# A three-branch decoder step on one core: the norms' factors spread by rounded high and low parts in place of four-byte products

## Chip, cores and metric

The kernel runs on one core of a Trainium2 chip. The metric is the device time of one execution in microseconds, lower is better.

## The reference, cut to what matters

One layer on 1024 prompt tokens and 8 sample tokens (1032 columns here), width 1024, everything in float32: a SwiGLU feed-forward block, an RWKV-7 and an S5 branch that are merged by gates, a second SwiGLU block, and a last norm. In front of each block stands the same norm:

```
def rmsnorm(x, g):
    xf = x.astype(jnp.float32)
    y = xf * lax.rsqrt(jnp.mean(xf * xf, axis=-1, keepdims=True) + NORM_EPS)
    return (y * g.astype(jnp.float32)).astype(x.dtype)

x = x + 0.5 * swiglu(rmsnorm(x, g_ffn1), ffn1_gate, ffn1_up, ffn1_down)
h = rmsnorm(x, g_mix);  proj = h @ w_in
...
x = x + 0.5 * swiglu(rmsnorm(x, g_ffn2), ffn2_gate, ffn2_up, ffn2_down)
y = rmsnorm(x, g_final)
```

## The kernel before

Activations lie with the 1024 channels on the partitions (8 tiles of 128) and the 1032 tokens along the row. **Large products.** A weight tile and an activation are each split into a part rounded to the format fp32r and the rest, also rounded; a product is hi*hi + hi*lo + lo*hi, three TensorE matmuls of fp32r (`product`, L199, its matmul on L213; L3476 in the second feed-forward block, L3495 and L3541 in its second half). One matmul has 344 columns (a third of the tokens, BLK), or 258 at L3476. POOL splits the weights (L179, L182; L3159), SyncE loads them.

**The norms.** A norm's factor 1/rms belongs to a token, and so is one number per column, the same on all 128 partitions. It is not applied to the input of the products but to their outputs, by VectorE, from the tile `rstd` (128 x 1032). It is made in four steps:

- ScalarE squares, VectorE adds up the eight tiles of squares in `ssum` (`square_sum`, L265).
- `sums_pe` (L276, matmul on L282): 12 four-byte matmuls with 86 columns of `ssum` as the weights and a column of ones (`seg`, column 2) as the moving operand. They turn the sums so that 86 tokens lie on 86 partitions: `ps[0:86, 6, 0:12]`.
- `rstd_small_dve` (L300): VectorE copies these 86x12 numbers into `small` and takes the reciprocal root in twelve more small steps (L230 to L241, three Newton steps), each waiting for the one before it; the result is `small[:, 1]`. Then it raises `rstd_small`.
- `rstd_pe` (L287, matmul on L293): 12 four-byte matmuls, each with one column of `small` repeated 128 times as the weights (86 rows x 128 columns) and the 86x86 identity `ident` as the moving operand; the result is the factor of 86 tokens on all 128 partitions. VectorE copies them to `rstd` in three pieces (`rstd_dve`, L309, copy on L313).

This happens three times: in front of the first feed-forward block (norm 0; TensorE comes to `rstd_pe` ahead of its fourth unit of weights, L581), in the projections (norm 1; inside the second unit, ahead of its sixth tile, L349 to L352), and in the second feed-forward block (norm 2; the root is written out by hand between other VectorE work, L3248 to L3263, and TensorE comes to `rstd_pe` after the fourth product of the second pair, L3483). The last norm has a copy of the step of its own (`factors_pe`, L3698, matmul on L3701) that reads `small` and `ident` too.

**Order.** Each engine runs one written-out list of instructions in order. TensorE's list is `sums_pe`, more large products, `rstd_pe`, more large products; a product's operands are waited for by semaphores (`w_split` from POOL, `set_free` from the engine that empties a PSUM bank). `seg` and `ident` are loaded by SyncE once near the start (L3601, L3602), with the semaphore `c_in`, for which TensorE waits on L574. `small` is 128 x 6 x 16 numbers; its rows 0 to 2 are the root's x, y and t, row 5 is the constant zero, and rows 3 and 4 are free.

Of the kernel before, what the change touches and what calls it, by code (L numbers as in the profile page):

```python
# [4 lines left out]
F32 = mybir.dt.float32  # L5
F32R = mybir.dt.float32r
I32 = mybir.dt.int32
ALU = mybir.AluOpType
# [4 lines left out]
P = 128  # L13
# [18 lines left out]
J = 16  # L32
SS = 86
NSS = TOK // SS
L8 = 8
GATES = 16
NORM_EPS = 1e-6
# [14 lines left out]
T_SEG = 7  # L52
# [45 lines left out]
def plan(nc, g):  # L98

    base = (nc.sbuf_base + 31) // 32 * 32  # L100
    g.limit = nc.sbuf_usable_end - base

    def at(name, off, shape, dt=F32):
        t = nc.alloc_sbuf_tensor_at(name, shape, dt, offset=base + off)
        return t, off + (int(np.prod(shape[1:])) * 4 + 31) // 32 * 32

    g.at = at
    o = 0

    g.wraw, o = at("wraw", o, [P, WSLOTS, 1024])  # L110
    g.whi_off = o
    g.whi, o = at("whi", o, [P, WSLOTS, 1024], F32R)
    g.wlo_off = o
    g.wlo, o = at("wlo", o, [P, WSLOTS, 1024], F32R)
    g.vec_off = o
    g.vec, o = at("vec", o, [P, NVEC])
    g.ident, o = at("ident", o, [P, P])
    g.seg, o = at("seg", o, [P, P])
    g.small, o = at("small", o, [P, 6, 16])
    g.zero = g.small[:, 5, 0:1]  # L120
    g.rstd, o = at("rstd", o, [P, TOK])
    g.s5p, o = at("s5_persistent", o, [P, 4, J])

    g.hhi, o = at("hhi", o, [P, DT, TOK], F32R)
    g.hlo, o = at("hlo", o, [P, DT, TOK], F32R)
    g.h_end = o
    g.x, o = at("x", o, [P, DT, TOK])
    g.x_end = o
    ga = max(FFN_GROUPS)
    g.ahi, o = at("ahi", o, [P, ga, TOK], F32R)  # L130
    g.alo, o = at("alo", o, [P, ga, TOK], F32R)
    g.first_raw = at("first_raw", o - 2 * TOK * 4, [P, 2, TOK])[0]
    g.tmp_off = o
    g.tmp, o = at("tmp", o, [P, 2, TOK])
    g.ssum, o = at("ssum", o, [P, TOK])
    assert o <= g.limit, (o, g.limit)
    g.ffn_end = o
    g.ps = nc.alloc_psum_tensor("ps", [P, 8, 512], F32)

    S = nc.alloc_semaphore  # L140
    g.w_in = [S("weights_in0"), S("weights_in1")]
    g.w_hi = S("weights_hi")
    g.first_set = S("first_steps")
    g.w_split = S("weights_split")
    g.unit_done = S("unit_done")
    g.set_free = [S("set_free0"), S("set_free1")]
    g.dve_s, g.act_s, g.pool_s = S("dve_steps"), S("act_steps"), S("pool_steps")
    g.x_in, g.c_in, g.out_done = [S(f"x_in{k}") for k in range(DT)], S("consts_in"), S("out_done")
    g.sq_ready, g.ssum_step, g.norm_ss = S("squares_ready"), S("square_sums"), S("norm_sums")
    g.rstd_small, g.rstd_b, g.rstd_ready = S("rstd_small"), S("rstd_broadcast"), S("rstd_ready")  # L150
    g.hhi_ready, g.h_ready = S("h_hi"), S("h_ready")
    g.silu_done, g.a_full, g.a_hi, g.a_ready = S("silu_done"), S("a_full"), S("a_hi"), S("a_ready")
    g.dve_n = g.act_n = g.pool_n = 0
    g.units = 0
    g.uses = [0, 0]
    g.norms = 0
    g.a_tiles = 0
# [80 lines left out]
def rsqrt(v, st, y, x, t, scale, eps, floor=None):  # L238

    if floor is None:  # L240
        st.do(v.tensor_scalar(x, x, scale, eps, ALU.mult, ALU.add))  # L241
    else:
        st.do(v.tensor_scalar(x, x, scale, floor, ALU.mult, ALU.max))
    rsqrt_steps(v, st, y, x, t)
# [31 lines left out]
def sums_pe(pe, g, n, ssum=None):  # L276

    pe.wait_ge(g.ssum_step, DT * (n + 1))
    if n:
        pe.wait_ge(g.rstd_ready, 3 * n)  # L280
    for j in range(NSS):
        last = pe.matmul(g.ps[0:SS, 6, j:j + 1], (g.ssum if ssum is None else ssum)[:, j * SS:(j + 1) * SS], g.seg[:, 2:3],  # L282
# [4 lines left out]
def rstd_pe(pe, g, n):  # L287

    pe.wait_ge(g.rstd_small, n + 1)
    for j in range(NSS):  # L290
        if j == 10:
            pe.wait_ge(g.rstd_ready, 3 * n + 1)
        last = pe.matmul(g.ps[:, 6 + (j // 5) % 2, (j % 5) * SS:(j % 5 + 1) * SS],  # L293
                         g.small[0:SS, 1, j:j + 1].to_broadcast([SS, P]), g.ident[0:SS, 0:SS],
                         start=True, stop=True)
        if j in (4, 9, 11):
            last.then_inc(g.rstd_b, 1)


def rstd_small_dve(v, g, st, n):  # L300

    v.wait_ge(g.norm_ss, n + 1)
    x, y, t = (g.small[0:SS, a, 0:NSS] for a in range(3))
    st.do(v.tensor_copy(x, g.ps[0:SS, 6, 0:NSS]))
    rsqrt(v, st, y, x, t, 1.0 / D, NORM_EPS)
    v.sem_inc(g.rstd_small, 1)


def rstd_dve(v, g, n):  # L309
# [25 lines left out]
def h_dve(v, g, gcol, n):  # L335

    for k in range(DT):
        h_lo(v, g, gcol, n, k)
    for k in range(DT):
        square_sum(v, g, n, k)  # L340
# [22 lines left out]
def ffn_block(nc, g, w_up, w_down, gcol, before=None, after=None, setup=None, ahead=None, loaded=False, normed=False,  # L363
# [24 lines left out]
    if block:  # L388
# [37 lines left out]
        def _(v):  # L426
            st = Steps(v, g.dve_s, g.dve_n)
            if not normed:
                h_dve(v, g, gcol, n0)
            rstd_small_dve(v, g, st, n0)  # L430
            rstd_dve(v, g, n0)
            v.wait_ge(g.rstd_ready, 3 * n0 + 3)
# [2592 lines left out]
def strassen_ffn(nc, g, w_up, w_down, gcol, n0, a_dram, x_dram, final, update, updated, block):  # L3025
# [187 lines left out]
    def _(v):  # L3213
        st = Steps(v, g.dve_s, g.dve_n)
# [15 lines left out]
        def first_pairs():  # L3230
            G, U = ([[halves(t[:, j, x]) for x in xa] for j in range(2)] for t in (g.gate, g.upv))
            R = [halves(g.rstd[:, x]) for x in xa]
            x, y, t = (g.small[0:SS, a, 0:NSS] for a in range(3))

            def add(pair, k, copy, out, where):
                done(v, 0, pair, k)
                g.st_copy.wait(v, 0, pair, copy)
                return v.tensor_tensor(out, two(where, pair), out, ALU.add)

            def newton():  # L3240
                st.do(v.scalar_tensor_tensor(t, y, -0.5, y, ALU.mult, ALU.mult))
                st.do(v.tensor_tensor(t, t, x, ALU.mult))
                st.do(v.scalar_tensor_tensor(y, t, 1.5, y, ALU.add, ALU.mult))

            for q in range(4):
                late("b22", g.x[:, 2 * q + 1, xa[1]], q)
            v.wait_ge(g.norm_ss, n0 + 1)
            st.do(v.tensor_copy(x, g.ps[0:SS, 6, 0:NSS]))  # L3248
            st.do(v.tensor_scalar(x, x, 1.0 / D, NORM_EPS, ALU.mult, ALU.add))
            on(add(0, 3, "p1", G[0][0], "y"))  # L3250
            on(add(0, 4, "p5", U[0][1], "x"))
            st.do(v.tensor_scalar(t.bitcast(I32), x.bitcast(I32), 1, None, ALU.logical_shift_right))
            st.do(v.tensor_scalar(y.bitcast(I32), t.bitcast(I32), -1.0, RSQRT_MAGIC, ALU.mult, ALU.add))
            newton()
            on(add(0, 5, "u2", G[0][1], "z"))
            newton()
            done(v, 0, 0, 6)
            on(v.tensor_copy(U[0][0], two("x", 0)))
            newton()
            v.sem_inc(g.rstd_small, 1)  # L3260
            add(1, 3, "p1", G[1][0], "y").then_inc(g.b_mixed, 1)
            rstd_dve(v, g, n0)
            v.wait_ge(g.rstd_ready, 3 * n0 + 3)  # L3263
            g.st_up.wait(v, 0, 0, "u1")
            on(v.tensor_tensor(G[0][0], G[0][0], R[0], ALU.mult))
            on(v.tensor_tensor(G[0][1], G[0][1], R[1], ALU.mult))
            on(v.tensor_tensor(U[0][1], U[0][1], R[1], ALU.mult))
            add(1, 4, "p5", U[1][1], "x").then_inc(g.b_mixed, 1)
            v.tensor_tensor(U[0][0], U[0][0], R[0], ALU.mult).then_inc(g.b_mixed, 1)
            v.wait_ge(g.b_mixed, 19)  # L3270
            g.st_copy.wait(v, 0, 0, "silu1")
            on(v.tensor_tensor(G[0][0], G[0][0], U[0][0], ALU.mult))
            g.st_up.wait(v, 0, 0, "u2m")
            g.st_copy.wait(v, 0, 0, "silu2")
            on(v.tensor_tensor(G[0][1], G[0][1], U[0][1], ALU.mult))
# [48 lines left out]
        for u in range(LAST):  # L3324
# [8 lines left out]
            if k < 6:  # L3333
                t = 6 * b + k
                hi, low, full = g.slot[DOWN_BLOCKS[b + 1][2][k]]
# [229 lines left out]
def build(nc, a, o):  # L3565

    g = Ctx()
# [20 lines left out]
    def first_loads(sp):  # L3588
        def unit(n):
            sp.dma_start(g.wraw[:, n, :], a["ffn1_up"][n]).then_inc(g.w_in[n], 16)  # L3590

        def odd_x(ks):
            for k in ks:
                sp.dma_start(g.x[:, k, :], a["x"][:, k, :]).then_inc(g.x_in[k], 16)

        unit(0)
        odd_x((1, 3, 5))
        unit(1)
        odd_x((7,))
        sp.wait_ge(g.hhi_ready, 1)  # L3600
        sp.dma_start(g.ident[:, :], a["tabs"][:, T_ID, :]).then_inc(g.c_in, 16)  # L3601
        sp.dma_start(g.seg[:, :], a["tabs"][:, T_SEG, :]).then_inc(g.c_in, 16)  # L3602
        sp.dma_start(g.braw[:, :, :, :], a["s5_b"]).then_inc(g.s5_in, 16)
        sp.dma_start(g.craw[:, :, :, :], a["s5_c"]).then_inc(g.s5_in, 16)

# [217 lines left out]
```

## Time and profile before

| | |
|---|---|
| median of 3 runs | 2463.25 us (2461.17 to 2464.54) |
| profiled execution, its own time | 2463.62 us |
| its span (first to last instruction) | 2461.8 us |
| TensorE (PE) busy | 2415.3 us, 98% of the span |
| VectorE (DVE) / ScalarE (ACT) / GpSimd (POOL) busy | 1282.6 / 579.2 / 1057.5 us |
| mean granted TensorE clock | 0.993 of 2.4 GHz |

The profile is of one execution. PE is TensorE's matmuls, PEld its loads of weights, which overlap with matmuls; neither duration is therefore the cost of an instruction. What an instruction costs TensorE is read from the distance between starts in the timeline.

### The profile page before, as it was taken

Reading aid. Unit: us, or ns where it says so; the run is one execution under the profiler, and the core shown is the slowest. Engines: PE = TensorE matmul, PEld = TensorE weight load, DVE = VectorE, ACT = ScalarE, POOL = GpSimd, SP = SyncE. Lnnn points to the kernel's source line nnn. Section 1 sums busy time; section 2 is a strip of 40 time slices with the busy share of each in tenths; the row PEclk is TensorE's granted clock in tenths of the full one; section 3 lists DMA queues with packets and bytes.
Section 4 is the critical chain, followed back from the end, with each engine's and each line's share of the span. In section 5 each row is a group of like instructions: output and inputs, shape, how many; then the busy total and the mean of one; then the engine's idle time right before and its main releaser. Section 6 shows DMA issues by size and latency. Waiting matters only on the chain. (4 is left out here: it accounts for less than half of the span.)

```text
span 2461.8 us, 50035 instructions
## 1 busy us (share of the span) xinstructions
PE 2415.3 (98%) x21418; PEld 2363.9 (96%) x21418; DVE 1282.6 (52%) x1843; ACT 579.2 (24%) x1084; POOL 1057.5 (43%) x604
## 2 busy tenths in 40 slices
PE   8999999999999999999998999999999999999998
PEld 8999999999999999999997888899999999999998
DVE  5851871671336255552466766566754444453225
ACT  4000010010011000011336676412433333341001
POOL 3434444334444344422340000254686868775550
PEclk9999999999999899999999999999999999999999
DMA  3111211211114432633451100072121212153211
GB/s 141 43 53 50 75 62 51 69 52 59 52 37 177 100 95 86 177 87 105 147 189 59 33 18 19 30 252 92 69 100 64 94 62 92 63 186 106 75 52 69
DMA packets 93733, 211.94 MB, mean 86 GB/s; under 512 B 16464, under 2 KB 42704, under 8 KB 92816
## 3 DMA queue, kind: packets, MB, share of 16 engines
q1 hardware_dynamic: 67184, 157.96, 19.7%
q10 hardware_dynamic: 26400, 51.82, 6.6%
q8 instruction: 115, 1.88, 0.3%
q14 instruction: 34, 0.28, 0.0%
HBM read 154.39 MB, written 54.20 MB: 85 GB/s over the span
## 5 line engine op out<-in xcount | busy, mean ns | idle before, releaser
L179 POOL TENSOR_TENSOR whi<-wraw,small 128x1024 fp32r<-128x1024 f32 (+3 forms) x136 | 232.5, 1710 | 846.0 <-PE ps L213 772.3
L213 PE MATMUL ps<-hhi,whi 128*128 128x344 f32 x1848 | 396.5, 323 | 0.0
L213 PE MATMUL ps<-hlo,whi 128*128 128x344 f32 x1848 | 393.2, 321 | 0.0
L213 PE MATMUL ps<-hhi,wlo 128*128 128x344 f32 x1848 | 391.3, 320 | 0.0
L182 POOL TENSOR_TENSOR wlo<-wraw,whi 128x1024 fp32r<-128x1024 f32 (+3 forms) x136 | 332.2, 2443 | 10.7
L213 PEld LDWEIGHTS ps<-hlo,whi 128*128 128x128 f32 x1848 | 313.8, 190 | 0.0
L213 PEld LDWEIGHTS ps<-hhi,whi 128*128 128x128 f32 x1848 | 310.9, 189 | 1.9 <-issue 0.7
L213 PEld LDWEIGHTS ps<-hhi,wlo 128*128 128x128 f32 x1848 | 309.2, 189 | 0.0
L3476 PE MATMUL ps<-t_hi,whi 128*128 128x258 f32 x704 | 143.8, 286 | 3.0 <-ACT ffn_gate L3383 1.0
L3476 PE MATMUL ps<-t_lo,whi 128*128 128x258 f32 x704 | 142.2, 283 | 0.0
L534 ACT ACTIVATE tmp<-tmp 128x1032 f32<-128x1032 f32 x22 | 23.5, 1068 | 504.2 <-DVE tmp L455 487.8
L3476 PE MATMUL ps<-t_hi,wlo 128*128 128x258 f32 x704 | 141.4, 282 | 0.0
L3159 POOL TENSOR_TENSOR wlo<-weights_sum,whi 128x512 fp32r<-128x512 f32 x66 | 91.8, 1391 | 52.6 <-ACT whi L3355 51.3
L3476 PEld LDWEIGHTS ps<-t_hi,whi 128*128 128x128 f32 x704 | 108.7, 189 | 4.9 <-POOL wlo L3159 1.7
L1773 POOL TENSOR_TENSOR sm_v<-sm_v,rw_e 128x2048 f32<-128x2048 f32 x1 | 3.6, 3620 | 252.7 <-DVEq L1537 252.7
L213 PE MATMUL ps<-ahi,whi 128*128 128x344 f32 x528 | 112.0, 320 | 0.0
L213 PE MATMUL ps<-alo,whi 128*128 128x344 f32 x528 | 111.8, 320 | 0.0
L213 PE MATMUL ps<-ahi,wlo 128*128 128x344 f32 x528 | 111.5, 319 | 0.0
L3476 PEld LDWEIGHTS ps<-t_lo,whi 128*128 128x128 f32 x704 | 109.0, 189 | 0.0
L3476 PEld LDWEIGHTS ps<-t_hi,wlo 128*128 128x128 f32 x704 | 109.0, 189 | 0.0
L492 DVE SCALAR_TENSOR_TENSOR x<-ps,x 128x1032 f32 x24 | 29.6, 1233 | 151.4 <-PE ps L213 151.4
L3476 PE MATMUL ps<-b_lo,whi 128*128 128x258 f32 x528 | 106.4, 283 | 0.0
(511 smaller groups left out, 5052.2 us busy)
## 6 DMA issues: line engine op xcount, KB each, us to landing
wraw<-ffn_up SPq DMA_DIRECT2D x44, 512.0 KB, 3.3
wraw<-ffn_down SPq DMA_DIRECT2D x40, 384.0 KB, 3.1
wraw<-ffn_up SPq DMA_DIRECT2D x11, 1024.0 KB, 4.9
weights_raw_b<-ffn_up SPq DMA_DIRECT2D x11, 1024.0 KB, 4.8
a_spilled<-ffn_gate SPq DMA_DIRECT2D x18, 516.0 KB, 2.7
a_raw<-a_spilled SPq DMA_DIRECT2D x18, 516.0 KB, 4.0
wraw<-w_mix SPq DMA_DIRECT2D x18, 512.0 KB, 3.4
gates<-gate_out ACTq DMA_DIRECT2D x16, 516.0 KB, 2.9
```

The lines of the kernel that those rows point to most:

```text
L179: pool.tensor_tensor(g.whi[:, s, 0:n], g.wraw[:, s, 0:n], g.zero.to_broadcast([P, n]), ALU.add).then_inc(g.w_hi, 1)
L182: pool.tensor_tensor(g.wlo[:, s, 0:n], g.wraw[:, s, 0:n], g.whi[:, s, 0:n].bitcast(F32), ALU.subtract).then_inc(g.w_split, 1)
L213: last = pe.matmul(g.ps[:, 3 * bank_set + b, 0:BLK], w[:, s, k * P:(k + 1) * P], x(k, b), start=(k == 0 and first), stop=(k == kt - 1 and ...
L492: v.scalar_tensor_tensor(xt, acc(g, j), 0.5, xt, ALU.mult, ALU.add)\
L534: act.activation(g.tmp[:, 0, :], g.tmp[:, 0, :], ACT.Silu).then_inc(g.silu_done, 1)
L1773: st.do(pool.tensor_tensor(V, V, over(E7[:, :, sample]), ALU.mult))
L3159: pool.tensor_tensor(ring(g.wlo, n), source(n), ring(g.whi, n).bitcast(F32), ALU.subtract).then_inc(g.st_lo, 1)
L3476: last = pe.matmul(g.ps[:, b0 + c, 0:QB], ring(w, r, k), x[:, k, c * QB:(c + 1) * QB], start=start and k == 0 and first, stop=k == DT // 2 ...
```

## The change

The factor is cut into a rounded high part and the rounded rest (`small_parts`, two VectorE instructions on 86x12 numbers behind the root), written as fp32r to the free rows 3 and 4 of `small`. `rstd_pe` issues two fp32r matmuls for each of the 12 pieces, high and low part, which accumulate in the same place, with an identity that VectorE has once copied to fp32r (`ident_r`, 128x86, ahead of the first norm's root, behind a wait for `c_in`). `seg` is stored and loaded with 72 columns in place of 128. `sums_pe` and the last norm's `factors_pe` are as before.

```
--- before.py
+++ after.py
@@ -32,6 +32,7 @@
 J = 16
 SS = 86
 NSS = TOK // SS
+SEG_COLS = 72
 L8 = 8
 GATES = 16
 NORM_EPS = 1e-6
@@ -115,11 +116,13 @@
     g.vec_off = o
     g.vec, o = at("vec", o, [P, NVEC])
     g.ident, o = at("ident", o, [P, P])
-    g.seg, o = at("seg", o, [P, P])
+    g.seg, o = at("seg", o, [P, SEG_COLS])
     g.small, o = at("small", o, [P, 6, 16])
     g.zero = g.small[:, 5, 0:1]
+    g.small_r = at("small_parts", o - (3 * 16 * 4 + 31) // 32 * 32, [P, 2, 16], F32R)[0]
     g.rstd, o = at("rstd", o, [P, TOK])
     g.s5p, o = at("s5_persistent", o, [P, 4, J])
+    g.ident_r, o = at("ident_rounded", o, [P, SS], F32R)
 
     g.hhi, o = at("hhi", o, [P, DT, TOK], F32R)
     g.hlo, o = at("hlo", o, [P, DT, TOK], F32R)
@@ -290,9 +293,10 @@
     for j in range(NSS):
         if j == 10:
             pe.wait_ge(g.rstd_ready, 3 * n + 1)
-        last = pe.matmul(g.ps[:, 6 + (j // 5) % 2, (j % 5) * SS:(j % 5 + 1) * SS],
-                         g.small[0:SS, 1, j:j + 1].to_broadcast([SS, P]), g.ident[0:SS, 0:SS],
-                         start=True, stop=True)
+        for part in range(2):
+            last = pe.matmul(g.ps[:, 6 + (j // 5) % 2, (j % 5) * SS:(j % 5 + 1) * SS],
+                             g.small_r[0:SS, part, j:j + 1].to_broadcast([SS, P]), g.ident_r[0:SS, 0:SS],
+                             start=part == 0, stop=part == 1)
         if j in (4, 9, 11):
             last.then_inc(g.rstd_b, 1)
 
@@ -303,7 +307,15 @@
     x, y, t = (g.small[0:SS, a, 0:NSS] for a in range(3))
     st.do(v.tensor_copy(x, g.ps[0:SS, 6, 0:NSS]))
     rsqrt(v, st, y, x, t, 1.0 / D, NORM_EPS)
+    small_parts(v, g, st, y)
     v.sem_inc(g.rstd_small, 1)
+
+
+def small_parts(v, g, st, y):
+
+    hi, lo = (g.small_r[0:SS, part, 0:NSS] for part in range(2))
+    st.do(v.tensor_copy(hi, y))
+    st.do(v.tensor_tensor(lo, y, hi.bitcast(F32), ALU.subtract))
 
 
 def rstd_dve(v, g, n):
@@ -427,6 +439,8 @@
             st = Steps(v, g.dve_s, g.dve_n)
             if not normed:
                 h_dve(v, g, gcol, n0)
+            v.wait_ge(g.c_in, 16 * 2)
+            st.do(v.tensor_copy(g.ident_r[:, :], g.ident[:, 0:SS]))
             rstd_small_dve(v, g, st, n0)
             rstd_dve(v, g, n0)
             v.wait_ge(g.rstd_ready, 3 * n0 + 3)
@@ -3257,6 +3271,7 @@
             done(v, 0, 0, 6)
             on(v.tensor_copy(U[0][0], two("x", 0)))
             newton()
+            small_parts(v, g, st, y)
             v.sem_inc(g.rstd_small, 1)
             add(1, 3, "p1", G[1][0], "y").then_inc(g.b_mixed, 1)
             rstd_dve(v, g, n0)
@@ -3599,7 +3614,7 @@
         odd_x((7,))
         sp.wait_ge(g.hhi_ready, 1)
         sp.dma_start(g.ident[:, :], a["tabs"][:, T_ID, :]).then_inc(g.c_in, 16)
-        sp.dma_start(g.seg[:, :], a["tabs"][:, T_SEG, :]).then_inc(g.c_in, 16)
+        sp.dma_start(g.seg[:, :], a["tabs"][:, T_SEG, 0:SEG_COLS]).then_inc(g.c_in, 16)
         sp.dma_start(g.braw[:, :, :, :], a["s5_b"]).then_inc(g.s5_in, 16)
         sp.dma_start(g.craw[:, :, :, :], a["s5_c"]).then_inc(g.s5_in, 16)
```

## Rows read from the trace of the kernel before

**Rows 1.** The page: busy time of each engine; the chain that ended last, by engine.

```profile
PE 2415.3 (98%) x21418; PEld 2363.9 (96%) x21418; DVE 1282.6 (52%) x1843; ACT 579.2 (24%) x1084; POOL 1057.5 (43%) x604
...
PE 32%; POOL 1%; DVE 1%; issue 0%; ACT 0%; DMA 0%; DVEq 0%; SPq 0%; POOLq 0%
```

**Rows 2.** One line's instructions, L293: count, ns min/median/max, starts.

```profile
L293 PEld LDWEIGHTS ps<-ident,small x72: 188/190/193, 47.7 to 1779.0; 86*128 86x128 f32 x72
L293 PE MATMUL ps<-ident,small x72: 238/275/276, 47.9 to 1779.1; 86*128 86x86 f32 x72
```

**Rows 3.** Timeline at norm 0: start us, us, what, count.

```profile
47.40 0.64 PE L213 MATMUL ps<-hhi,wlo 128*128 128x344 f32 x3
...
47.71 2.81 PEld L293 LDWEIGHTS ps<-ident,small 86*128 86x128 f32 x24
...
49.15 0.61 DVE L313 COPY rstd<-ps 128x430 f32<-128x430 f32 x1 [5.72 <-PE ps L293]
...
51.02 0.63 PE L213 MATMUL ps<-hlo,whi 128*128 128x344 f32 x3
```

**Rows 4.** Timeline: steady matmuls of 344 columns, of 258 columns.

```profile
41.24 0.64 PE L213 MATMUL ps<-hlo,whi 128*128 128x344 f32 x3
...
45.97 0.64 PE L213 MATMUL ps<-hhi,wlo 128*128 128x344 f32 x3
...
1766.02 0.40 PE L3476 MATMUL ps<-b_lo,whi 128*128 128x258 f32 x2
...
1776.36 0.40 PE L3476 MATMUL ps<-b_hi,wlo 128*128 128x258 f32 x2
```

**Rows 5.** Groups by form: weight loads of 128 (fp32r, four-byte), 86, 64 and 32 columns; mean ns.

```profile
L213 PEld LDWEIGHTS ps<-hhi,whi 128*128 128x128 f32 x1848 | 310.9, 189 | 1.9 <-issue 0.7
...
L293 PEld LDWEIGHTS ps<-ident,small 86*128 86x128 f32 x72 | 8.4, 190 | 0.0
...
L282 PEld LDWEIGHTS ps<-seg,ssum 128*86 128x86 f32 x72 | 5.9, 157 | 0.0
...
L2379 PEld LDWEIGHTS ps<-rw_t,rw_x 64*64 64x64 f32 x1280 | 47.8, 134 | 0.0
...
L2471 PEld LDWEIGHTS ps<-rw_e,rw_tab 128*32 128x32 f32 x72 | 1.5, 108 | 0.7 <-issue 0.2
```

**Rows 6.** Timeline at L2521: four-byte, 128 weight columns, 8 moving columns.

```profile
1602.41 0.97 PEld L2521 LDWEIGHTS ps<-rw_norm,rw_sel 128*128 128x128 f32 x8
...
1602.52 0.96 PE L2521 MATMUL ps<-rw_norm,rw_sel 128*128 128x8 f32 x8
...
1603.30 0.19 PEld L2667 LDWEIGHTS ps<-ya_hi,whi 128*128 128x128 f32 x1
```

**Rows 7.** Timeline: end of the root, VectorE's wait and TensorE's arrival, norms 0, 1, 2.

```profile
40.86 0.17 DVE L304 COPY small<-ps 86x12 f32<-86x12 f32 x1 [5.43 <-PE ps L282]
...
43.27 0.17 DVE L235 SCALAR_TENSOR_TENSOR small<-small 86x12 f32<-86x12 f32 x1
...
781.62 2.41 POOL L182 TENSOR_TENSOR wlo<-wraw,whi 128x1024 fp32r<-128x1024 f32 x1
...
781.81 2.26 DVE L234 TENSOR_TENSOR small<-small 86x12 f32<-86x12 f32 x1
...
784.10 0.17 DVE L235 SCALAR_TENSOR_TENSOR small<-small 86x12 f32<-86x12 f32 x1
...
786.27 2.81 PEld L293 LDWEIGHTS ps<-ident,small 86*128 86x128 f32 x24
...
1769.08 0.17 DVE L3243 SCALAR_TENSOR_TENSOR small<-small 86x12 f32<-86x12 f32 x1
...
1776.59 2.81 PE L293 MATMUL ps<-ident,small 86*128 86x86 f32 x24
```

**Rows 8.** DMA issues up to 45 us: KB each, us to landing; and SyncE's timeline.

```profile
seg<-tabs SPq DMA_DIRECT2D x1, 64.0 KB, 6.9
...
9.38 0.43 SPq L3602 DMA_DIRECT2D seg<-tabs  x1
```

More of the change, by code:

```diff
@@ L34 @@
 NSS = TOK // SS
+SEG_COLS = 72
 L8 = 8
@@ L117, in plan @@
     g.ident, o = at("ident", o, [P, P])
-    g.seg, o = at("seg", o, [P, P])
+    g.seg, o = at("seg", o, [P, SEG_COLS])
     g.small, o = at("small", o, [P, 6, 16])
     g.zero = g.small[:, 5, 0:1]
+    g.small_r = at("small_parts", o - (3 * 16 * 4 + 31) // 32 * 32, [P, 2, 16], F32R)[0]
     g.rstd, o = at("rstd", o, [P, TOK])
     g.s5p, o = at("s5_persistent", o, [P, 4, J])
+    g.ident_r, o = at("ident_rounded", o, [P, SS], F32R)
     g.hhi, o = at("hhi", o, [P, DT, TOK], F32R)
@@ L292, in rstd_pe @@
             pe.wait_ge(g.rstd_ready, 3 * n + 1)
-        last = pe.matmul(g.ps[:, 6 + (j // 5) % 2, (j % 5) * SS:(j % 5 + 1) * SS],
-                         g.small[0:SS, 1, j:j + 1].to_broadcast([SS, P]), g.ident[0:SS, 0:SS],
-                         start=True, stop=True)
+        for part in range(2):
+            last = pe.matmul(g.ps[:, 6 + (j // 5) % 2, (j % 5) * SS:(j % 5 + 1) * SS],
+                             g.small_r[0:SS, part, j:j + 1].to_broadcast([SS, P]), g.ident_r[0:SS, 0:SS],
+                             start=part == 0, stop=part == 1)
         if j in (4, 9, 11):
@@ L305, in rstd_small_dve, with small_parts @@
     rsqrt(v, st, y, x, t, 1.0 / D, NORM_EPS)
+    small_parts(v, g, st, y)
     v.sem_inc(g.rstd_small, 1)
+def small_parts(v, g, st, y):
+    hi, lo = (g.small_r[0:SS, part, 0:NSS] for part in range(2))
+    st.do(v.tensor_copy(hi, y))
+    st.do(v.tensor_tensor(lo, y, hi.bitcast(F32), ALU.subtract))
 def rstd_dve(v, g, n):
@@ L429, in _ @@
                 h_dve(v, g, gcol, n0)
+            v.wait_ge(g.c_in, 16 * 2)
+            st.do(v.tensor_copy(g.ident_r[:, :], g.ident[:, 0:SS]))
             rstd_small_dve(v, g, st, n0)
@@ L3601, in first_loads @@
         sp.dma_start(g.ident[:, :], a["tabs"][:, T_ID, :]).then_inc(g.c_in, 16)
-        sp.dma_start(g.seg[:, :], a["tabs"][:, T_SEG, :]).then_inc(g.c_in, 16)
+        sp.dma_start(g.seg[:, :], a["tabs"][:, T_SEG, 0:SEG_COLS]).then_inc(g.c_in, 16)
         sp.dma_start(g.braw[:, :, :, :], a["s5_b"]).then_inc(g.s5_in, 16)
```

1 line of the change is left out of this document (added).

## The prediction

> **What bounds the kernel now.** I read first the page: TensorE is busy for 98% of the span, no other engine for more than 52%, and the chain that ended last names no engine but TensorE with more than 1% [rows 1]. So a microsecond of TensorE's list is a microsecond of the kernel, nearly everywhere, and work on VectorE counts only where TensorE waits for it. Then the line that is changed, L293: its 3 x 12 four-byte matmuls stand in the trace as 72 loads of weights and 72 matmuls, two records for each [rows 2]. Third the timeline around them, for what they cost: TensorE never stops before, in or after them. Fourth the groups by form and the neighbours of L293 in kind, to see what sets the cost of one record: its moving columns, its passes, or its weights.
>
> **The cost of the step now.** At norm 0 a group of three matmuls starts at 47.40, and after those three, the 24 records and three more the next group starts at 51.02 [rows 3]. Six matmuls of 344 columns take 6 x 157.7 ns = 0.95 us, where 157.7 ns is the steady distance (45.97 - 41.24 us over ten groups of three) [rows 4]. That leaves 3.62 - 0.95 = 2.67 us for 24 records, 111 ns each. Norms 1 and 2 look alike, so the whole step costs 3 x 2.67 = 8.0 us, 0.33% of the span. More than that cannot be won at this line.
>
> **Part 1, the products: 12 four-byte ones become 24 rounded ones.** Every fp32r matmul of the trace is one record, so there are 24 records before and 24 after, each with weights of 128 columns and 86 moving columns. Before, the two records of a product already write the same place one after the other, so that the accumulation is nothing new. The question is the price of a rounded record, and none with so few moving columns is in the trace. I bound it:
>
> - Low end, if moving columns set it: 344 columns take 157.7 ns and 258 take 120.2 ns (1776.36 - 1766.02 us over 43 pairs) [rows 4], which is 0.437 ns per column; drawn on to 86 columns it gives 45 ns, and the three norms would save 3 x 24 x (111 - 45) = 4.8 us.
> - High end, if a narrow rounded matmul were worked like a whole four-byte product, in four passes: 4 x 86 x 0.437 ns = 150 ns, and the 7.4 ns by which 258 columns stand over 258 x 0.437 ns, make 158 ns; the three norms would lose 3 x 24 x (158 - 111) = 3.4 us.
> - In the middle stands the load of the weights. A record of L2521 has 128 columns of weights and only 8 moving columns, and still eight of them take 1603.30 - 1602.41 = 0.89 us, 111 ns each [rows 6]: the same as at L293 with 86. So at 111 ns it is not the moving columns that TensorE waits for, nor passes over them, but the 128 columns of weights. A load grows with its columns: 108, 134, 157 and 190 ns for 32, 64, 86 and 128, some 0.85 ns a column, and it takes as long in fp32r (189 ns) as in four bytes (190 ns) [rows 5]. In the large products it is hidden under 344 or 258 moving columns, here nothing is long enough to hide it.
>
> I take 111 ns, the value of the nearest row (same weights, few moving columns, and equal load times in both formats): 3 x 24 x (111 - 111) = 0. The moving part shrinks under a load that does not.
>
> Two rules of the Trainium skill stand against each other here. "FP8 and Floating Point Precision", TensorE Precision Notes, counts four passes for true FP32; by passes alone 12 x 4 x 86 columns become 24 x 86, half the columns, and for that the change would be a gain. "TensorE: Matmul & The Clock Gate", LDWEIGHTS, says that a load takes its columns divided by 1.2 GHz, whatever the rows: an estimate of 107 ns for 128 columns, in both formats, and by it nothing is gained; the slope of the loads [rows 5] and the 111 ns [rows 6] agree with the second.
>
> **Part 2, two more VectorE steps behind each root.** A step of the root takes 0.17 us and the next one starts 0.20 us later (13 steps from 40.86 to 43.27 at norm 0) [rows 7], so the two add 0.40 us. TensorE arrives at its step 4.3 us after the root at norm 0 (47.71 against 43.44), 2.0 us at norm 1 (786.27 against 784.27), 7.3 us at norm 2 (1776.59 against 1769.25) [rows 7]. What hides them is the large products that TensorE does between; the price is 0, and 0.40 us each if that cover were gone. Queued behind them on VectorE are the copies of L313, which wait for TensorE anyway, and at norm 2 one addition that waits for TensorE's fourth product. POOL has nothing running right after 784.03, so I take the short duration at norm 1.
>
> **Part 3, the identity's copy and the narrower table.** VectorE copies 128x86 numbers once. No row has this copy; it lies between the 0.17 us of an 86x12 step and the 0.61 us of L313's copy of 430 columns [rows 3]; I take 0.3 us. It stands behind the sums of squares, where VectorE sits idle for 5.43 us until 40.86 [rows 7]. Its wait for `c_in` is over long before: the issue of `seg` starts at 9.38 and it lands 6.9 us later [rows 8]. Price 0. `seg` moves 36 KB in place of 64 KB, and nobody waits for it: 0. The buffers behind `small` shift by 128 bytes (224 fewer, 352 more): 0.
>
> **Sum.** Against the profiled execution's own 2463.6 us: 0 + 0 + 0 us. It stands 0.4 us above the median of the runs, 2463.25 us, so I forecast 2463.2 us.
>
> **Rivals.**
>
> - Moving columns decide after all (rounded weights load behind the matmul before them as fast as the columns pass). For it: in the large products 0.437 ns a column explains both widths. Against it: a load of 128 columns takes 189 ns in fp32r as well [rows 5]. Price up to -4.8 us, 2458.5 us. The skill's page "TensorE: Matmul & The Clock Gate" (Back-to-back issue gap) gives 81 ns for a load and a matmul of 128 columns, as measured there; by that the three norms would save an estimated 2.2 us.
> - Slower: a narrow rounded matmul is worked in four passes, at L293, 158 ns a record. It costs from 111 ns on, because below that the load covers it. For it: nothing in the trace shows a rounded matmul under 258 columns. Against it: at 258 and 344 columns it is plainly one pass. Price +3.4 us, 2466.7 us.
> - Slower, second: at norm 1 VectorE's small steps are stretched while POOL splits weights, as one was, 2.26 us in place of 0.17 beside L182's 2.41 us [rows 7]. If both new steps met that, TensorE would stand for 2 x 2.26 - 2.0 = 2.5 us: 2465.8 us. In the run shown POOL was done before the root was.
> - The change doesn't do what it says: if the compiler still made two records of each rounded matmul, 48 records of 111 ns would add 3 x 24 x 0.111 = 8.0 us: 2471.2 us. Against it: one record for each matmul at L213 and L3476.
>
> **How the numbers follow.** A measurement of this kernel tells from no change what is over 0.2%, 4.9 us. Load-bound, no change: 0.68. Moving columns decide, wholly or in part: 0.14. Four passes: 0.10. Late steps at norm 1: 0.04. Two records each: 0.04. The first two rivals alone end within 0.2%, even at their ends; only together with the runs' own spread of 3 us do they cross it. So same is 0.88; faster 0.06, from the low end of the first rival; slower 0.06, from the last rival and the high end of the second. The range reaches over most of both bounds, with a microsecond of the runs' spread: 2459.0 to 2466.8 us.
>
> **What would show it.** After: 24 records in each of three places again, the same 2.67 us between the large products, loads of 190 ns, and next to them matmuls whose own duration is shorter, since fewer passes go through. Right: distance of 108 to 114 ns. 45 to 100 ns: the first rival. 140 to 160 ns: the second. A wait of TensorE for VectorE ahead of L293 at norm 1: the third. 48 records: the fourth. VectorE: two more steps of 0.17 us after each root and one copy near 35.5 us. I am wrong if the step differs by over 0.5 us at a norm, or if TensorE's first waits in the second feed-forward block move with it.

## The result, and the profile after

The changed kernel takes 2468.61 us (median of 12 runs, 2464.93 to 2469.57) against 2462.72 us for the kernel before in the same rounds (12 runs, 2458.67 to 2467.61): ratio 1.0021, 95% interval 1.0013 to 1.0029. By the medians it is slower by 5.9 us, by the ratio by some 5 us, where no change was forecast, and the median lies outside the forecast range of 2459.0 to 2466.8 us. A second measurement on another occasion gave 1.0012 (1.0003 to 1.0021). The profiled execution took 2468.22 us, its span is 2466.4 us, 4.6 us more than before.

The page after, in the two rows that answer to [rows 1]:

```profile
PE 2418.9 (98%) x21418; PEld 2368.1 (96%) x21418; DVE 1284.3 (52%) x1850; ACT 579.4 (23%) x1084; POOL 1054.3 (43%) x604
...
PE 32%; DVE 1%; POOL 1%; issue 0%; ACT 0%; DMA 0%; DVEq 0%; SPq 0%; POOLq 0%
```

TensorE has the same 21418 matmuls, VectorE seven instructions more (one copy and 3 x 2 steps), TensorE is busy 3.6 us longer, and the chain names nothing new. The changed line, where before [rows 2] stood (count, ns min/median/max, starts):

```profile
L297 PEld LDWEIGHTS ps<-ident_rounded,small_parts x72: 188/192/192, 47.2 to 1782.5; 86*128 86x128 f32 x72
L297 PE MATMUL ps<-ident_rounded,small_parts x72: 203/287/289, 47.3 to 1782.6; 86*128 86x86 f32 x72
```

and the timeline around it at norm 0 (start us, us, what), with the two new VectorE steps and the identity's copy:

```profile
35.22 1.90 DVE L443 CAST ident_rounded<-ident 128x86 fp32r<-128x86 f32 x1
...
43.01 0.17 DVE L317 CAST small_parts<-small 86x12 fp32r<-86x12 f32 x1
43.22 0.17 DVE L318 TENSOR_TENSOR small_parts<-small,small_parts 86x12 fp32r<-86x12 f32 x1
...
46.84 0.64 PE L216 MATMUL ps<-hhi,wlo 128*128 128x344 f32 x3
...
47.32 2.77 PE L297 MATMUL ps<-ident_rounded,small_parts 86*128 86x86 f32 x24
...
50.47 0.64 PE L216 MATMUL ps<-hlo,whi 128*128 128x344 f32 x3
```

Worked as for [rows 3]: 50.47 - 46.84 = 3.63 us, less 0.95 us for six large matmuls, is 2.68 us for 24 records, 112 ns each, against 2.67 us before. Norm 2 gives 1782.68 - 1780.08 = 2.60 us from the step's first matmul to the next product's, before 1779.19 - 1776.59 = 2.60 us. L297 has no idle time of TensorE ahead of it in any of the three places. So the step itself costs what it did, and the 4.6 us of the span are not in it.

They are in what TensorE's clock is granted. Over the whole span it is 0.991 after and 0.993 before, and a time at 0.5 costs half of itself: 0.009 x 2466.4 / 0.5 = 44 us at half clock, 22 us lost, against 0.007 x 2461.8 = 17 us lost before; the difference is the span's, within the rounding of the clock's third digit. Added up stretch by stretch from the two traces, 22.9 us are lost after and 18.4 us before: 4.5 of the 4.6 us. Three stretches of 3.4 us at half clock stand in the trace after and not in the one before (the others give back 0.6 us), at 789.0, 1243.0 and 1263.5 us. The one at 1243.0 has nothing to do with the change: two later traces of the kernel before have it too, at 1239.5 and 1244.2 us. The first of the three stands right behind the rounded step of norm 1. The timeline of TensorE there:

```profile
785.93 2.77 PE L297 MATMUL ps<-ident_rounded,small_parts 86*128 86x86 f32 x24
788.52 0.79 PE L216 MATMUL ps<-hhi,whi 128*128 128x344 f32 x3
789.11 1.06 PE L216 MATMUL ps<-hlo,whi 128*128 128x344 f32 x3
...
791.69 0.98 PE L216 MATMUL ps<-hlo,whi 128*128 128x344 f32 x3
792.51 0.64 PE L216 MATMUL ps<-hhi,wlo 128*128 128x344 f32 x3
```

Groups of three matmuls of 344 columns start 0.86 us apart in place of 0.47 us, three groups in a row from 789.11 to 791.69. The windows say why (length in us; busy us and count of PE, PEld, DVE, ACT and POOL; then the granted clock, the DMA engines' busy share and GB/s; the kernel before first, then after):

```profile
788.90:792.30 3.40, 3.40 (x25) 3.40 (x24) 2.82 (x6) 0.00 (x0) 0.00 (x0) 1.00 0.92 382
```

```profile
788.90:792.30 3.40, 3.40 (x15) 3.40 (x14) 2.21 (x5) 0.00 (x0) 0.00 (x0) 0.52 0.75 308
```

TensorE is busy for all of the 3.40 us in both, but its clock is the lower level, 1.2 GHz, in the changed kernel: 15 matmuls start in place of 25, 10 x 0.158 us = 1.6 us lost. What TensorE's rows show before the fall is no idle time: they show the 24 rounded records, back to back.

### The profile page after: what moved, and what is told of

Same layout as the page of the kernel before. It is cut to its first block and busy times, and to the rows that moved or that the text cites. A ratio compares the mean times of both kernels' runs of the same rounds, so it can differ in the third digit from the quotient of the medians.

```text
span 2466.4 us, 50043 instructions
## 1 busy us (share of the span) xinstructions
PE 2418.9 (98%) x21418; PEld 2368.1 (96%) x21418; DVE 1284.3 (52%) x1850; ACT 579.4 (23%) x1084; POOL 1054.3 (43%) x604
## 5 line engine op out<-in xcount | busy, mean ns | idle before, releaser
L185 POOL TENSOR_TENSOR wlo<-wraw,whi 128x1024 fp32r<-128x1024 f32 (+3 forms) x136 | 326.2, 2399 | 10.7
```

The costliest lines, as they stand in the source:

```text
L185: pool.tensor_tensor(g.wlo[:, s, 0:n], g.wraw[:, s, 0:n], g.whi[:, s, 0:n].bitcast(F32), ALU.subtract).then_inc(g.w_split, 1)
```

## The experiments

Every kernel ran beside the kernel before on the same chip; "n" is the number of runs of each kernel. The rounds of one set share the runs of before.

### First set: is it the change, and is it the products?

**after_again** and **before_again** repeat the two kernels unchanged. **four_byte_again** puts back the four-byte products alone, and keeps the rounded parts, the rounded identity and the narrower table:

```
-        for part in range(2):
-            last = pe.matmul(..., g.small_r[0:SS, part, j:j + 1].to_broadcast([SS, P]),
-                             g.ident_r[0:SS, 0:SS], start=part == 0, stop=part == 1)
+        last = pe.matmul(..., g.small[0:SS, 1, j:j + 1].to_broadcast([SS, P]),
+                         g.ident[0:SS, 0:SS], start=True, stop=True)
```

**twice_as_wide** keeps the rounded pairs and reads the identity twice in 10 of the 12 pieces, so that 172 columns pass under a load (the second copy lands in the place that the next piece overwrites):

```
+        twice = 1 if j % 5 == 4 else 2
...
-                             ... g.ident_r[0:SS, 0:SS],
+                             ... g.ident_r[0:SS, 0:SS].rearrange("p (a c) -> p a c", a=1).to_broadcast([SS, twice, SS]),
```

> The changed kernel, unchanged, once more, for a second trace. Clock theory: the step of L297 costs the same 2.67 us in each norm, and the granted clock falls to half behind at least one of the three steps again, 3.4 us each, a loss of 1.7 us each; the kernel is 4 to 6 us slower than before. Side-parts theory (the two VectorE steps, the copy, the moved buffers): the falls behind the three steps are chance; the loss is in the stretch from 1240 to 1280 us again, 3 to 5 us. Chance theory: the traces differ from each other by as much as from before.

> The kernel before, for a second trace of it. Clock theory: no fall of the granted clock behind any of the three steps at L293. Chance theory: falls there as often as in the changed kernel, and a span up to 4 us longer than in the first trace.

> The changed kernel with the 12 four-byte products of before put back; the two VectorE steps, the rounded identity's copy, the narrower table and the moved buffers stay. Clock theory: no fall of the clock behind the three steps, and the time of before within 0.1%. Side-parts theory: as slow as the changed kernel, 0.2% over before.

> The changed kernel with each rounded matmul made 172 columns wide in place of 86 (the identity read twice; the second copy lands where the next product writes anyway), save at the two that close a bank. As many loads of 128 columns, but as many moving columns as the four-byte products had passes over. Clock theory: the step still takes 2.6 to 2.8 us, the load of weights hides the added columns, and the clock no longer falls behind it: the time of before within 0.1%. Side-parts theory: no better than the changed kernel, 0.2% over before.

Measured, against 2462.11 us (n = 27): after_again 2467.38 us (n = 11), 1.0012 (1.0003 to 1.0021); four_byte_again 2464.54 us (n = 11), 1.0007 (0.9998 to 1.0016); twice_as_wide 2465.1 us (n = 11), 1.0010 (1.0001 to 1.0019); before_again, one run, 2462.2 us, span 2460.4 us. The same window behind norm 1 as above, of after_again, four_byte_again and twice_as_wide in turn:

```profile
788.90:792.30 3.40, 3.40 (x14) 3.40 (x14) 2.01 (x5) 0.00 (x0) 0.00 (x0) 0.50 0.58 234
```

```profile
788.90:792.30 3.40, 3.40 (x23) 3.40 (x22) 1.84 (x4) 0.00 (x0) 0.00 (x0) 1.00 0.60 245
```

```profile
788.90:792.30 3.40, 3.40 (x24) 3.40 (x24) 2.47 (x6) 0.00 (x0) 0.00 (x0) 1.00 0.92 381
```

The fall comes with the narrow rounded products and goes with either remedy: four-byte records of the same length, or rounded ones with twice the columns. But both remedies still lie 2.4 and 3.0 us above before in the median, the first of them with an interval that holds 1. So there may be a second part.

### Second set: four times the dose, and another shape

**rounded_x4**, **four_byte_x4** and **wide_x4** issue each product of the step four times over (96 records a norm, the same result written again), in the three forms; the changed line is `for part in (0, 1) * 4:` in the first and the last, and `for _ in range(4):` around the four-byte product. **wide_diagonal** turns the product round: the weights are a column of ones repeated, the moving operand is diag(hi) and diag(lo), which VectorE makes from the identity, and six matmuls with 430, 430 and 172 columns replace 24 with 86; at norm 1 the step also stands one tile later:

```
-    for j in range(NSS):
+    for i, (c0, c1) in enumerate(((0, RB), (RB, 2 * RB), (2 * RB, TOK))):
...
+        for part, x in enumerate(diag_parts(g, n)):
+            last = pe.matmul(g.ps[:, 6 + i % 2, 0:c1 - c0], g.small_r[0:SS, 0, 12:13].to_broadcast([SS, P]),
+                             x[0:SS, c0:c1], start=part == 0, stop=part == 1)
```

> The changed kernel with each pair of rounded matmuls issued four times over: 96 records a norm, 107 us... to be exact 96 x 111 ns = 10.7 us in each norm at the full clock. Clock theory: the granted clock falls to half inside the step in all three norms and comes back only behind it; records may take longer while it is low. Side-parts theory: no fall there that the four-byte counterpart does not show too.

> The same with the four-byte products of before, each issued four times: 96 records a norm, 96 x 111 ns = 10.7 us. Clock theory: 24 us over before (3 x 8.0) and no fall of the granted clock inside or behind the three steps, since twice as many columns pass in each record.

> The same with the rounded matmuls of 172 columns, each pair four times: 96 records a norm at 111 ns again, as many columns passing as in the four-byte counterpart. Clock theory: no fall inside the steps, and 1.7 us or more shorter for each norm than the narrow rounded ones. If the format and not the columns mattered, the clock falls as in the narrow ones.

> The roles changed: VectorE multiplies the identity by the high and by the low factors into two 86x1032 tiles (high in rstd, low in the tile of the sums; two more VectorE steps of some 1.2 us behind the root), and TensorE spreads them with ones as weights: 6 rounded matmuls of 430, 430 and 172 columns a norm in place of 24 of 86; at norm 1 the step stands one tile later. Load theory: 2064 columns x 0.437 ns + 6 x 14 ns = 1.0 us a norm in place of 2.67, and no fall of the clock behind it: 5 us under before, 8 to 10 under the changed kernel. If the moving columns had been the cost, it would be as long as the 24 narrow ones (2064 columns each way) and nothing would be gained.

Measured (against 2463.24 us, n = 15): 2513.09, 2488.11 and 2491.47 us in one run each; wide_diagonal 2462.96 us (n = 11), 1.0000 (0.9991 to 1.0009). TensorE's step at norm 0 and the product after it, in rounded_x4:

```profile
47.13 16.58 PE L297 MATMUL ps<-ident_rounded,small_parts 86*128 86x86 f32 x96
...
63.50 1.21 PE L216 MATMUL ps<-hhi,whi 128*128 128x344 f32 x3
```

and in four_byte_x4:

```profile
46.83 10.85 PE L297 MATMUL ps<-ident,small 86*128 86x86 f32 x96
57.47 0.72 PE L216 MATMUL ps<-hhi,whi 128*128 128x344 f32 x3
```

96 records take 10.64 us with four bytes, 111 ns each, and 16.37 us rounded, 171 ns each. The windows behind norms 0 and 1 hold the reason; rounded_x4:

```profile
50.00:70.00 20.00, 20.00 (x99) 20.00 (x99) 6.24 (x7) 2.13 (x2) 1.70 (x1) 0.57 0.09 27
800.00:825.00 25.00, 25.00 (x138) 25.00 (x137) 3.59 (x8) 0.00 (x0) 0.00 (x0) 0.66 0.30 119
```

four_byte_x4:

```profile
50.00:70.00 20.00, 20.00 (x148) 20.00 (x148) 8.51 (x9) 3.21 (x3) 2.22 (x2) 1.00 0.09 27
800.00:825.00 25.00, 25.00 (x171) 25.00 (x171) 7.06 (x14) 0.00 (x0) 9.10 (x6) 1.00 0.23 86
```

wide_x4:

```profile
50.00:70.00 20.00, 20.00 (x128) 20.00 (x128) 7.63 (x8) 3.19 (x3) 1.27 (x1) 0.83 0.08 27
800.00:825.00 25.00, 25.00 (x180) 25.00 (x179) 7.66 (x15) 0.00 (x0) 6.70 (x6) 1.00 0.24 87
```

With the long dose the clock falls at all three norms with narrow rounded records (17.1, 17.1 and 13.7 us at half clock, together 47.9, so 24 us lost, of the 25.0 us by which rounded_x4's span of 2511.3 stands over four_byte_x4's 2486.3), at none with four-byte ones, and at one of three with the wide ones (0.83 above). This is the cleanest row of the study. A load-bound stretch hides from the busy share what passes under the loads: all three forms are "busy" throughout. The clock told them apart. Before the falls TensorE ran rounded records of 86 columns; with rounded records of twice the columns, or with four-byte records of 86, it kept its clock in five of six steps.

The Trainium skill, "TensorE: Matmul & The Clock Gate" (Part 1: The HAM clock gate), has the clock set by "how busy the PE has been recently". If busy is read as in the profile's rows, the trace differs: TensorE's records stand without a gap from 47.13 to 63.50, PE is busy for 20.00 of 20.00 us, and the clock falls all the same. But the ends of matmul records are modelled, and no row shows how much of that time the array itself was at work under the loads. So the runs show which form of the step lets the clock fall; that the array stands idle under the loads is a reason that was only argued.

wide_diagonal also settles what the step waits for. Its timeline at norm 0:

```profile
47.04 0.36 PE L303 MATMUL ps<-rstd_rounded,small_parts 86*128 86x430 f32 x1
...
48.30 0.35 PE L303 MATMUL ps<-rstd_rounded,small_parts 86*128 86x172 f32 x1 [0.30 <-DVE rstd L334]
48.48 0.27 PE L303 MATMUL ps<-ssum_rounded,small_parts 86*128 86x172 f32 x1
...
48.59 0.67 PE L218 MATMUL ps<-hhi,whi 128*128 128x344 f32 x3
```

From its first matmul to the next product pass 1.55 us, where the changed kernel takes 49.91 - 47.32 = 2.59, with exactly as many moving columns in all (2 x 1032) and 6 loads for 24. The loads were the cost, and a quarter of the loads shortens the step by 1.0 us at norms 0 and 1 and by 0.8 us at norm 2, though now TensorE waits 0.30 to 0.54 us for VectorE to empty the bank. Yet the kernel is no faster than before, where 5 us under it were expected: these 3 us are taken back outside of the steps, which the next sets follow.

### Third set: the side parts by themselves

**layout_only** is the kernel before with `seg` at 72 columns and an `ident_r` that nobody uses, so that the buffers behind `small` stand where they do after. **steps_only** is the kernel before with the two VectorE steps behind each root, unused. **diagonal_old_places** is wide_diagonal with the buffers in their old places. **before_third** is before once more.

```
layout_only, on the kernel before
+SEG_COLS = 72
-    g.seg, o = at("seg", o, [P, P])
+    g.seg, o = at("seg", o, [P, SEG_COLS])
+    g.ident_r, o = at("ident_rounded", o, [P, SS], F32R)
-        sp.dma_start(g.seg[:, :], a["tabs"][:, T_SEG, :]).then_inc(g.c_in, 16)
+        sp.dma_start(g.seg[:, :], a["tabs"][:, T_SEG, 0:SEG_COLS]).then_inc(g.c_in, 16)

steps_only, on the kernel before (in rstd_small_dve, and behind norm 2's root)
+    small_parts(v, g, st, y)

diagonal_old_places, on wide_diagonal
-    g.seg, o = at("seg", o, [P, SEG_COLS])
+    g.seg, o = at("seg", o, [P, P])
-    g.ident_r, o = at("ident_rounded", o, [P, SS], F32R)
...
```

> The kernel before with nothing but the new places: the table seg 72 columns wide and loaded so, the (unused) rounded identity behind it, and so every large buffer 128 bytes further on. Products, root and VectorE's steps as before. Places theory: the stretch from 1240 to 1280 us shows the second fall of the clock and TensorE's longer waits for POOL as in all five kernels with the moved buffers, 2 to 3 us over before. Chance theory: as before within 0.05%.

> The kernel before with nothing but the two VectorE steps behind each root (their result unused; no moved buffers, no identity copy). They are hidden, so all theories but one say as before within 0.05%; if the two steps were what disturbs the stretch from 1240 to 1280 us, 2 to 3 us over before.

> The wide diagonal with the buffers where they were before (table of 128 columns, no rounded identity). Places theory: 3 to 4 us under before, since the step is 1.1 us shorter in each norm and the stretch from 1240 to 1280 us is as before. Chance theory, or the gain is taken back in that stretch by waits for POOL and the transfers: the time of before within 0.1%, as with the moved buffers.

> The kernel before, for a third trace: how many falls of the clock lie between 1235 and 1280 us (none in the first trace, one in the second; the kernels with moved buffers have two). Places theory: none or one. Chance theory: as many as two.

Measured, against 2462.16 us (n = 27), each n = 11 but the last: layout_only 2463.87 us, 1.0007 (0.9998 to 1.0016); steps_only 2464.15 us, 1.0007 (0.9998 to 1.0016); diagonal_old_places 2462.28 us, 1.0002 (0.9993 to 1.0011); before_third, one run, 2463.6 us. No verdict by time: each interval holds 1. The traces tell more. In the stage near 1260 us, where TensorE runs close behind POOL's splitting of `w_b`, the waits (engine line waited for: us in total, times, longest us) are, before:

```profile
POOL whi L179 <- DMA wraw<-w_b: 18.6, 5, 4.9
...
PE ps L213 <- POOL wlo L182: 1.1, 3, 0.5
```

and after:

```profile
POOL whi L182 <- DMA wraw<-w_b: 22.5, 5, 6.6
...
PE ps L216 <- POOL wlo L185: 2.4, 2, 1.9
```

One load of `w_b` makes the difference. The DMA view of the stretch in which it is on its way, before (queues; then KB and us from issue to landing):

```profile
q1 hardware_dynamic: 417, 1.05, 62.8%
q10 hardware_dynamic: 144, 0.53, 23.9%
issues: line engine op xcount, KB each, median us to landing
...
wraw<-w_b SPq DMA_DIRECT2D x1, 256.0 KB, 5.4
```

and after:

```profile
q10 hardware_dynamic: 144, 0.53, 18.2%
q14 instruction: 1, 0.01, 0.3%
issues: line engine op xcount, KB each, median us to landing
...
wraw<-w_b SPq DMA_DIRECT2D x1, 256.0 KB, 7.1
```

The load takes 7.1 us in place of 5.4, POOL waits 6.6 us for it in place of 4.9, and TensorE in turn 1.9 us for POOL in place of 0.5. Right behind that stop the clock falls once more: window 1263.50 to 1266.90 after, and then before:

```profile
1263.50:1266.90 3.40, 3.40 (x12) 3.40 (x13) 2.84 (x7) 3.33 (x10) 1.41 (x2) 0.50 1.03 289
```

```profile
1263.50:1266.90 3.40, 3.40 (x25) 3.40 (x24) 2.87 (x5) 1.83 (x5) 2.12 (x2) 1.00 0.86 294
```

One row stands only in the view after: a transfer of queue 14, "instruction", about 8 KB (34 of them move 0.28 MB over the whole kernel); by the queue's name it is a fetch of instructions. layout_only has the load at 5.2 us and no such stop, so the moved buffers are not it. after_again has it at 7.1 us, four_byte_again and twice_as_wide at 7.2, wide_diagonal at 7.4, diagonal_old_places at 6.9, all with the queue 14 transfer inside the load's flight; in steps_only it starts 0.6 us behind the landing, and the load takes 6.2 us. That made a theory: the added VectorE instructions move a later fetch of instructions in time, and here it moves into a load for which TensorE has no slack.

### Fourth set: move the fetch, change nothing else

One-column memsets of `rstd` (all overwritten later) in VectorE's idle time ahead of norm 0's root make its program longer: 11 and 40 on the kernel before, 28 on the changed one, 24 on wide_diagonal.

```
before_pad11, on the kernel before (before_pad40: 40; after_pad28 and diagonal_pad24 alike)
+            for i in range(11):
+                v.memset(g.rstd[:, i:i + 1], 0.0)
             rstd_small_dve(v, g, st, n0)
```

> The kernel before with 11 one-column VectorE memsets in its idle time ahead of norm 0's root, nothing else. Fetch theory: the fetch of instructions that came 9.7 us after the issue of the load of w_b near 1252 us moves into that load (about 4 us after the issue, as in the changed kernel), the load lands after 7 us in place of 5.4, TensorE stops 2 us or more near 1260 us, a second fall of the clock follows, and the median is 1.5 to 3 us over before. Places or chance theory: load, stop and time as before.

> The same with 40 memsets (2.8 us of VectorE's 5.4 us of idle time). Fetch theory: the fetch comes ahead of the load of w_b, the load lands after 5.2 to 5.7 us, no stop near 1260 us over 1 us, the time of before within 0.05%. If more instructions as such cost time, it is slower than with 11.

> The changed kernel with 28 such memsets. Fetch theory: the load of w_b near 1254 us lands after 5.2 to 5.7 us again, the stop near 1260 us and the fall behind it are gone, and the median is 2 to 3 us under the changed kernel; the fall behind norm 1's rounded matmuls stays (1.7 us), so it is still 1.5 to 3 us over before. Places or chance theory: no better than the changed kernel.

> The wide diagonal with 24 such memsets. Fetch theory: the stop of 2.5 us near 1260 us and its fall are gone and the 1.1 us a norm are kept: 2 to 4 us under before. Otherwise 0 to 1 us from before, as without them.

Measured, against 2462.77 us (n = 33), each n = 11: before_pad11 2464.09 us, 1.0007 (0.9998 to 1.0016); before_pad40 2462.11 us, 0.9998 (0.9989 to 1.0007); after_pad28 2465.44 us, 1.0014 (1.0005 to 1.0023); diagonal_pad24 2463.5 us, 1.0003 (0.9994 to 1.0012). The same load in before_pad11:

```profile
q14 instruction: 1, 0.01, 0.3%
issues: line engine op xcount, KB each, median us to landing
...
wraw<-w_b SPq DMA_DIRECT2D x1, 256.0 KB, 7.2
```

and in before_pad40:

```profile
q10 hardware_dynamic: 144, 0.53, 24.3%
issues: line engine op xcount, KB each, median us to landing
...
wraw<-w_b SPq DMA_DIRECT2D x1, 256.0 KB, 5.3
```

Eleven memsets of no use, 1200 us ahead, make the kernel before show the late load, a wait of TensorE for POOL of 2.0 us at its longest, and a fall of the clock behind it; forty put the fetch outside and all three are gone, as in after_pad28 (load 5.8 us, longest wait 0.6 us, no fall there). Over all twenty traces of this study: with the fetch inside the flight the load takes 6.9 to 7.4 us (10 of 10), without it 5.2 to 6.2 us (10 of 10). This holds for that one load only. The next load of `w_b` has such a fetch inside in every trace and takes 3.8 to 4.8 us, and later ones reach 7 us without one (7.0 us for the load of 1269.57 in the kernel before). How a few KB could delay 256 KB by 1.7 us is not in the trace: that the fetch, and not something else that the longer list moves, delays the load is argued, and stays open. The fall behind the stop comes in most traces that have the stop (not in after_again and diagonal_old_places), and in none without it. In the medians the effect is 2.0 us between the two padded kernels, within the uncertainty of either; before_pad11 was expected 1.5 to 3 us over before, and came 1.3 us over it.

diagonal_pad24 removes the late load (5.5 us, wait 0.6) from the shorter step and is still at 1.0003, not under before. Its span, 2461.2 us, is 1.6 us under wide_diagonal's 2462.8. So where the 3 us of the shorter step go is only partly shown. The clocks of all runs (see the sum in medians below) give one part: over the 33 runs of the three versions with the wide diagonal 19.5 us are lost to the clock on average, against 18.5 us in 121 runs of the kernel before. That is 1.0 us; some goes into the late load, and the rest stays open. No version beat the kernel before by what can be measured.

### Last set: the two causes apart, in medians

**after_pad28_again** repeats the padded changed kernel, **four_byte_pad28** is the same with the four-byte products of the first set's diff.

> The changed kernel with 28 one-column VectorE memsets ahead of norm 0's root, as in after_pad28: VectorE's program is longer, so that the instruction fetch near 1258 us lies ahead of the w_b load that starts at 1252.6 us. Two-cause theory: the narrow rounded products of norm 1 still cost one fall of the granted clock to 0.5 for 3.4 us at 788.9 us (1.7 us), and the late load, its stop of TensorE and the fall behind it stay away: 2464 to 2466 us, 1.0008 to 1.0014, clearly under the changed kernel's 1.0021. Rival (the padding changes nothing, the trace seen before was chance): 2467 to 2469 us, load 7.1 us, stop of 2.2 us near 1260.

> The same kernel with the padding, but the four-byte products put back in place of the rounded pairs (the rounded parts and the rounded identity are still made, and not used). Two-cause theory: both causes are gone, no fall at 788.9 us and no fetch within the w_b load, so that it is 1.7 us under after_pad28_again in the median and 0 to 1 us over the kernel before: 2462 to 2464 us, 1.0000 to 1.0004. Rival (the granted clock at norm 1 is not set by the products): a fall at 788.9 us here too, and a median that equals after_pad28_again's within 0.5 us.

Measured, against 2462.7 us (n = 19): 2466.94 us (n = 9), 1.0021 (1.0011 to 1.0031), and 2463.37 us (n = 11), 1.0003 (0.9994 to 1.0012). The window behind norm 1, of the first and then of the second:

```profile
788.90:792.30 3.40, 3.40 (x14) 3.40 (x14) 2.34 (x6) 0.00 (x0) 0.00 (x0) 0.53 0.50 200
```

```profile
788.90:792.30 3.40, 3.40 (x24) 3.40 (x23) 1.66 (x4) 0.00 (x0) 0.00 (x0) 1.00 0.85 346
```

The rival, equal medians, is out: with the fetch out of the way in both, the rounded products alone cost 3.6 us. That is more than the 1.7 us expected of one fall. after_pad28_again lies above the expected 2464 to 2466 us and just under the 2467 to 2469 us of its own rival, that the padding changes nothing; its trace speaks against that rival (load 6.2 us, longest wait 1.0 us, no fall near 1260 us), its time does not. four_byte_pad28 came as expected.

### The sum in medians

- Rounded against four-byte products: all 23 runs of the changed kernel have the median 2468.1 us, four_byte_again 2464.5; with padding, 2466.7 (20 runs) against 2463.4. That is 3.5 and 3.3 us.
- The fetch's place: 2468.1 against 2466.7, 2464.5 against 2463.4, and before_pad11 against before_pad40: 1.3, 1.2 and 2.0 us. Each alone is within the noise. The first pair does not hold up in other measures: its means differ by 0.6 us, and its ratios to before (1.0021 and 1.0012 against 1.0014 and 1.0021) do not tell the two apart. And layout_only and steps_only, whose traces have no late load, lie 1.7 and 2.0 us above before, as far as before_pad11 does. So the price of the fetch's place is argued, not shown.
- What is left: four_byte_pad28 over before, 0.7 us, not told from zero.

3.4 + 1.3 + 0.7 = 5.4 us, against the 5.9 and 5.3 us of the two measurements; the medians come from different occasions, so that it comes out so well is in part luck. Only the first term is shown.

Why do the products cost twice what the one fall in the traces costs? Each run has its span and its mean granted clock (to three digits) on record, and (1 - clock) x span is what it lost to the clock. The average is 21.4 us over the 43 runs with narrow rounded products (changed kernel and its padded form) and 18.5 us over the 22 runs of their four-byte twins. These 2.9 us (standard error 0.6 us) are nearly all of the 3.1 us between the mean times, 2467.2 and 2464.0 us. So the products' cost is clock and nothing else that can be told from zero. Where the part beyond the fall of 1.7 us stands stays open. The four-byte twins lose the same 18.5 us as the kernel before (121 runs) and are still 1.4 us slower in the mean, 2464.0 against 2462.6 us: what the side parts cost is, on average, not clock but longer waits or work; no run takes it apart further.

## Why the prediction was wrong, point by point

**The cost of the step: right.** "Right: distance of 108 to 114 ns" was the bound, 112 ns came. Loads of 192 ns, 24 records in each of three places, TensorE waiting for nobody ahead of them. The low end (45 ns) and with it the first rival, the high end of four passes (158 ns), and the last rival's 48 records are all excluded by the rows of L297, and wide_diagonal showed the reason by experiment: fewer loads, same columns, shorter.

**Part 1, "3 x 24 x (111 - 111) = 0": the term that failed.** The sentence "The moving part shrinks under a load that does not" was true of the step's time, and was taken to mean that nothing changes. But behind the narrow rounded records the granted clock fell to 0.5, and behind the four-byte records of the same pace it did not. The prediction priced a record in nanoseconds and named the clock nowhere, although the table of the profile before had it at 0.993: the kernel before already lost some 17 us to falls, and one more of the shortest length seen, 3.4 us, costs 1.7 us. The term was put at 0 and measured 3.3 to 3.6 us, 1.7 us of it in a fall that each of the four traces of this form shows.

**Part 2, two steps a norm: right in place, wrong in price.** The steps take 0.17 us and start 0.21 us apart (43.01, 43.22), and at norm 1 they are done at 784.20, 1.7 us ahead of TensorE's arrival at 785.93. One of norm 2's took 1.23 us, hidden as well. The third rival, 2.26 us twice, did not occur. But "the price is 0" looked only for who waits for the steps, not for what a longer instruction list moves: with 11 instructions more on VectorE's list the load near 1252 us took 7.2 us in place of 5.4, and in the trace of the changed kernel TensorE waited 1.9 us for what hung on it, with a fall behind. In medians that may be 1.2 to 2.0 us, which is not told from zero. "I am wrong if the step differs by over 0.5 us at a norm, or if TensorE's first waits in the second feed-forward block move" looked in neither of the two places.

**Part 3: the copy was mis-sized, without effect.** 0.3 us were estimated, 1.90 us measured (35.22; a POOL instruction of 2.71 us began at 34.34, and no trace has the copy without one beside it), well inside the idle time until the root begins at 40.39; it lay in VectorE's idle time as said. The buffers' move is not told from zero (layout_only).

**Range and chances.** The range was built from one family of unknowns, the nanoseconds of a record, and all the rivals on the slower side were such sizes. A cause outside of the step had no share, and neither had the clock. What came, 1.0021, lies at the limit of 0.2% up to which the prediction called two kernels the same, so its 0.88 for the same time was not far off; that the row "load-bound, no change" held for the step and not for the kernel is the failure.

## What to carry to other kernels

Where loads of weights set the pace, as at L297, narrowing or cheapening what passes under them gained nothing and lost clock: use the room under the load (wider or fewer products) or leave the four-byte product, and compare the granted clock window by window before comparing durations. When an edit adds instructions that hide perfectly, look for tight transfers far behind it, and try a few dummy instructions more before blaming the edit's content. Where one trace differs from another by 2 us, count the falls first.

## What was not expected of the hardware

- The granted clock fell to 0.5 with no gap in TensorE's records, behind 24 to 96 load-bound fp32r records of 86 columns: in 4 of 4 traces behind norm 1 with the narrow rounded step (x24), in none of 13 traces with another form of it; at all three norms with 96 records. Why norms 0 and 2 escape with 24 is open.
- A transfer of the queue "instruction" inside the flight of one 256 KB load goes with 6.9 to 7.4 us for it in place of 5.2 to 6.2, in twenty of twenty traces, and instructions added to VectorE's list 1200 us earlier move it in or out. Other loads of the same tensor do not follow this.
- fp32r with 128 weight columns loads no faster than four bytes: 192 ns against 190, and 112 against 111 ns from record to record.
